# Attention on pairs of heads with features on partitions, and pooling moved to the second projections

## The reference

```python
def gqa_attend(qb, k, v):
    s = jnp.einsum('bqhgd,bkhd->bhgqk', qb, k, preferred_element_type=jnp.float32) * HEAD_DIM ** -0.5
    p = jax.nn.softmax(s, axis=-1)
    return jnp.einsum('bhgqk,bkhd->bqhgd', p.astype(v.dtype), v)
...
    mix = jnp.concatenate([pool_mixer(p, w_pool, s_pool),
                           gla_output(o_gl, gg, g_gla, x.dtype),
                           latent_attention(ql, k_all, v_all)], axis=-1) @ w_out
```

## Time and profile before

| what | us |
|---|---|
| median of 3 runs | 2187.87 |
| lowest, highest | 2180.58, 2188.46 |
| the profiled execution | 2186.37 |
| its span on the core | 2184.6 |
| PE busy (share) | 1962.4 (90%) |
| DVE, ACT, POOL busy | 1141.4, 908.6, 318.5 |

### The profile page before, as it was taken

One profiled execution on the slowest core, in us unless ns is written; L12 is line 12 of the kernel. 1 busy time (PEld: TensorE's weight loads), 2 busy tenths in 40 slices (PEclk: granted clock), 3 DMA queues, 4 the chain that ended last, 5 costly groups with the idle time before them and its releaser, 6 DMA issues.

```text
span 2184.6 us, 28958 instructions
## 1 busy us (share of the span) xinstructions
PE 1962.4 (90%) x12175; PEld 1679.3 (77%) x12175; DVE 1141.4 (52%) x1623; ACT 908.6 (42%) x1404; POOL 318.5 (15%) x359
## 2 busy tenths in 40 slices
PE   4888778999999999869989977988899999988999
PEld 2766457788888888745788967878789978868997
DVE  2544447545466455564355545764355546565553
ACT  3543334344445544533354534433244435434443
POOL 1011013211131122120121110021200004300000
PEclk8998688999999999977789988989899999989999
DMA  7445253453546566432345533420055554503554
GB/s 266 138 155 192 95 195 97 155 164 132 167 157 212 193 211 197 137 114 78 122 146 187 181 127 98 134 77 20 25 164 182 185 184 163 184 20 116 179 187 136
DMA packets 217869, 320.59 MB, mean 147 GB/s; under 512 B 8454, under 2 KB 123850, under 8 KB 217356
## 3 DMA queue, kind: packets, MB, share of 16 engines
q1 hardware_dynamic: 212532, 308.96, 42.9%
q0 software_dynamic: 1744, 6.03, 0.8%
q10 hardware_dynamic: 3464, 3.75, 0.5%
HBM read 317.68 MB, written 1.05 MB: 146 GB/s over the span
## 4 chain that ended last, share of the span: by engine, by line
PE 74%; DVE 12%; ACT 6%; DMA 3%; issue 3%; POOL 2%; SPq 0%; POOLq 0%; ACTq 0%; DVEq 0%
PE ps L69 70%; DVE WLO L86 3%; PE ps L77 3%; DVE AR L96 2%; ACT WHI L80 2%; DVE AR L86 2%; DMA RAW<-in_w_mod_dram 1%; ACT AR L80 1%; POOL SM L86 1%; ACT PMD L80 1%; DMA RAW<-in_w_in_dram 1%; DVE SM L99 1%; ACT XR L80 1%; ACT TH L80 1%; POOL XR L86 1%
## 5 line engine op out<-in xcount | busy, mean ns | idle before, releaser
L86 DVE TENSOR_TENSOR WLO<-RAW,WHI 128x1024 fp32r<-128x1024 f32 (+3 forms) x506 | 591.4, 1211 | 426.0 <-ACT WHI L80 425.9
L80 ACT ACTIVATE WHI<-RAW 128x1024 fp32r<-128x1024 f32 (+3 forms) x506 | 488.7, 1015 | 388.0 <-PE ps L69 316.3
L69 PE MATMUL ps<-TH,WHI 128*128 128x256 f32 x1664 | 482.8, 290 | 24.9 <-DVE WLO L86 17.1
L69 PE MATMUL ps<-TL,WHI 128*128 128x256 f32 x1664 | 477.5, 287 | 0.0
L69 PE MATMUL ps<-TH,WLO 128*128 128x256 f32 x1664 | 477.4, 287 | 0.0
L69 PE MATMUL ps<-WHI,ARR 128*128 128x512 f32 x1120 | 357.6, 395 | 2.6 <-DVE ARR L86 1.5
L69 PEld LDWEIGHTS ps<-TH,WHI 128*128 128x128 f32 x1664 | 326.5, 196 | 34.9 <-issue 22.5
L69 PEld LDWEIGHTS ps<-TL,WHI 128*128 128x128 f32 x1664 | 326.7, 196 | 0.2
L69 PEld LDWEIGHTS ps<-TH,WLO 128*128 128x128 f32 x1664 | 326.1, 196 | 0.0
L69 PE MATMUL ps<-WHI,TH 128*128 128x512 f32 (+3 forms) x624 | 246.4, 395 | 29.8 <-DVE WLO L86 23.4
L69 PEld LDWEIGHTS ps<-WHI,ARR 128*128 128x128 f32 x1120 | 211.7, 189 | 55.2 <-issue 8.9
(11 more groups left out here) (170 smaller groups left out, 2025.0 us busy)
## 6 DMA issues: line engine op xcount, KB each, us to landing
RAW<-in_w_mod_dram SPq DMA_DIRECT2D x48, 1024.0 KB, 5.3
RAW<-in_w_up_dram SPq DMA_DIRECT2D x48, 1024.0 KB, 5.4
RAW<-in_w_down_dram SPq DMA_DIRECT2D x48, 1024.0 KB, 5.2
RAW<-in_ffn_w_in_dram SPq DMA_DIRECT2D x44, 1024.0 KB, 5.1
RAW<-in_w_in_dram SPq DMA_DIRECT2D x20, 1024.0 KB, 5.3
RAW<-in_ffn_w_out_dram SPq DMA_DIRECT2D x20, 1024.0 KB, 5.1
RAW<-in_dil_w_in_dram SPq DMA_DIRECT2D x18, 1024.0 KB, 5.0
RAW<-in_gdn_w_in_dram SPq DMA_DIRECT2D x16, 1024.0 KB, 5.8
```

The source lines that it names most:

```text
L69: return Made(None if self.eng is None else self.eng.matmul(o, l, r, start=start, stop=stop))
L80: return Made(None if self.eng is None else self.eng.activation(o, i, f, **k))
L86: return Made(None if self.eng is None else self.eng.tensor_tensor(o, a, b, op))
```

## The change

- Attention goes by pairs of heads (v = 0 and 1, the two key heads) in 8 steps plus a tail of 4. The two scores of a pair are issued one behind the other on the two halves of the array's rows. For sequence 0 both go into one bank (256 keys each), so the second waits for the first; one maximum and one copy then serve the pair. For sequence 1 they have a bank each.
- The product with the values is turned over: 64 value columns are stationary and the 128 transposed exps move, so that the result has features on partitions, the two heads of a pair on the two halves of the array's columns. The transposes `at` are gone. The reciprocal sums, which now must lie along the free axis, are spread by 8 matmuls per query tile (key `rs`, `ps<-CF,SM` 64x128), copied by ACT into `attended`, and multiplied in by DVE; ACT and DVE split the result as before.
- The output weights' lower 512 rows must be in the order of the new partitions: their tile of `w_out` is loaded by two transfers of 64 partitions each.
- Pooling's second product takes all four 64x64 quarters in one bank, and DVE and ACT work on 128 partitions at once (2 scalings, 1 split each, where there were 4 and 2).
- In `common_order` both poolings of layer 0 begin in the second projections (three of four steps there, the fourth first in the next stage), attention (0, 0) has 12 of its 36 steps there, and attention (0, 1) is `slow`.

The core of the diff, 8 columns of indentation taken off:

```diff
@@ -341,8 +341,14 @@
-        src = src[128 * t.k0:128 * (t.k0 + t.nk), t.c0:t.c0 + t.n].rearrange("(k p) n -> p k n", p=128)
-        sp.dma(t.of(t.raw), src).then_inc(w_land[t.i % NRAW], t.i)
+        src = src[128 * t.k0:128 * (t.k0 + t.nk), t.c0:t.c0 + t.n]
+        if (t.name, t.k0) == ("w_out", 4):
+            for v in range(2):
+                sp.dma(t.of(t.raw)[64 * v:64 * v + 64], src[256 * v:256 * v + 256].rearrange("(a d) n -> d a n", a=4)).then_inc(
+                    w_land[t.i % NRAW], t.i)
+        else:
+            sp.dma(t.of(t.raw), src.rearrange("(k p) n -> p k n", p=128)).then_inc(w_land[t.i % NRAW], t.i)
@@ -738,6 +744,7 @@
+PTBOTH = AR[:, 9984:11008].rearrange("p (v n) -> p v n", v=2)
@@ -966,128 +973,176 @@
...
+STEPS = [(qt, a) for qt in range(2) for a in range(4)]
+TAIL = 4
+def last_of(step):
+    return divmod(step, 4)[0] if 0 <= step < len(STEPS) and step % 4 == 3 else None
...
+def att_key(kind, l, sq, step, v):
+    return kind, l, sq, step, v * sq
+def att_of(kind, l, sq, step, v):
+    b = banks.of(att_key(kind, l, sq, step, v))
+    return b if sq == 1 else b[:, 256 * v:256 * v + 256]
+def att_take(kind, l, sq, step, v):
+    if v == 0 or sq == 1:
+        banks.take(att_key(kind, l, sq, step, v), aring)
+        wait_free(att_key(kind, l, sq, step, v))
+    return att_of(kind, l, sq, step, v)
+def att_pb(sq, step, v):
+    if sq == 0:
+        return PBb[step % 3][:, 256 * v:256 * v + 256], (step - 3, v)
+    return PBb[(2 * step + v) % 3], divmod(2 * step + v - 3, 2)
...
+    nk = 2 + 2 * sq
+    for step in range(len(STEPS) + TAIL):
+        if step < len(STEPS):
+            qt, a = STEPS[step]
+            pe.wait_ge(act_pj, ("qt", l, 2 * sq + qt))
...
+            for v in range(2):
+                p = slice(64 * v, 64 * v + 64)
+                b = att_take("s", l, sq, step, v)
+                if (sq, v) == (0, 1):
+                    pe.wait_ge(pe_at, ("s", l, sq, step, 0))
+                pe.matmul(b, QT[sq][p, a, 128 * qt:128 * qt + 128], KT[p, 0:128 * nk], True, True).then_inc(pe_at, ("s", l, sq, step, v))
...
+        if 0 <= u < len(STEPS):
+            qt, a = STEPS[u]
+            key = ("o", l, 2 * sq + qt)
+            if a == 0:
+                banks.take(key, oring)
+                wait_free(key)
+            b = banks.of(key)
+            for e in (act_at, dve_at):
+                if ("p", l, sq, u) in e.at:
+                    pe.wait_ge(e, ("p", l, sq, u))
...
+                for v in range(2):
+                    m = pe.matmul(b[64 * v:64 * v + 64, 128 * a:128 * a + 128], UA[:, i, 64 * v:64 * v + 64],
+                                  PTb[v][:, 128 * i:128 * i + 128], i == 0, i == nk - 1)
...
+        yield
+        u = step - 1
+        if 0 <= u < len(STEPS):
+            for v in range(2):
+                b = att_take("pt", l, sq, u, v)
+                pe.wait_ge(act_at, ("e", l, sq, u, v))
+                for i in range(nk):
+                    m = pe.transpose(b[:, 128 * i:128 * i + 128], att_pb(sq, u, v)[0][:, 128 * i:128 * i + 128], IDN)
+                m.then_inc(pe_at, ("pt", l, sq, u, v))
+        yield
+        if (i := last_of(step - 1)) is not None:
+            ti = 2 * sq + i
+            b = banks.take(("rs", l, ti), ring)
+            wait_free(("rs", l, ti))
+            pe.wait_ge(dve_at, ("rc", l, ti))
+            for h in range(8):
+                p, a = slice(64 * (h // 4), 64 * (h // 4) + 64), h % 4
+                m = pe.matmul(b[p, 128 * a:128 * a + 128], s_at[i][:, 16 + h:17 + h].broadcast_to([128, 64]), IDN, True, True)
+            m.then_inc(pe_at, ("rs", l, ti))
+        yield
+def act_exp(l, sq, step, v):
+    qt, a = STEPS[step]
+    h = 4 * v + a
+    to, (u, uv) = att_pb(sq, step, v)
+    act.wait_ge(dve_at, ("mx", l, sq, step, v * sq))
+    if u >= 0:
+        act.wait_ge(pe_at, ("pt", l, sq, u, uv))
+    free = [("free", att_key("s", l, sq, step, v))] if sq == 1 or v == 1 else []
+    act.act(to, att_of("s", l, sq, step, v), ACT.Exp, bias=s_at[qt][:, h:h + 1], accum_out=s_at[qt][:, 8 + h:9 + h]).then_inc(
+        act_at, ("e", l, sq, step, v), *free)
...
+    for step in range(len(STEPS) + TAIL):
+        if step < len(STEPS):
+            act_exp(l, sq, step, 0)
+            if sq == 0:
+                act_exp(l, sq, step, 1)
+        yield
+        if sq == 1 and step < len(STEPS):
+            act_exp(l, sq, step, 1)
+        u = step - 1
+        if 0 <= u < len(STEPS) and (sq == 1 or u % 2 == 0):
+            free = ("free", att_key("pt", l, sq, u, 0))
+            act.wait_ge(pe_at, ("pt", l, sq, u, 1 - sq))
+            if u >= 1:
+                act.wait_ge(pe_at, ("o", l, sq, u - 1))
+            if sq == 1:
+                act.act(PTb[0], banks.of(("pt", l, sq, u, 0)), ACT.Copy).then_inc(act_at, free, ("p", l, sq, u))
+            else:
+                act.act(PTBOTH[:, :, 0:256], banks.of(("pt", l, sq, u, 0)).rearrange("p (v n) -> p v n", v=2), ACT.Copy).then_inc(
+                    act_at, free, ("p", l, sq, u))
+        yield
+        if (i := last_of(step - 1)) is not None:
+            ti = 2 * sq + i
+            act.wait_ge(pe_at, ("rs", l, ti))
+            act.act(attended(l, ti), banks.of(("rs", l, ti)), ACT.Copy).then_inc(act_mx, ("free", ("rs", l, ti)), ("rs", l, ti))
+        if (i := last_of(step - 3)) is not None:
+            ti = 2 * sq + i
...
+            act.wait_ge(dve_mx, ("ao", l, ti))
+            act.act(MH[:, 4:8, 128 * ti:128 * ti + 128], h4(attended(l, ti)), ACT.Copy).then_inc(act_mx, ("at", l, ti))
...
+    for step in range(len(STEPS) + TAIL):
+        if step < len(STEPS):
+            qt, a = STEPS[step]
+            mx = s_at[qt][:, 0:8].rearrange("p (v a) -> p v a", v=2)[:, :, a]
+            dve.wait_ge(pe_at, ("s", l, sq, step, 1 - sq))
+            if sq == 0:
+                b = banks.of(("s", l, sq, step, 0)).rearrange("p (v n) -> p v n", v=2)
+                dve.reduce(mx, b, ALU.max, negate=True).then_inc(dve_at, ("mx", l, sq, step, 0))
+            else:
+                dve.reduce(mx[:, 0:1], banks.of(("s", l, sq, step, 0)), ALU.max, negate=True).then_inc(dve_at, ("mx", l, sq, step, 0))
+                dve.wait_ge(pe_at, ("s", l, sq, step, 1))
+                dve.reduce(mx[:, 1:2], banks.of(("s", l, sq, step, 1)), ALU.max, negate=True).then_inc(dve_at, ("mx", l, sq, step, 1))
+        if (i := last_of(step - 1)) is not None:
+            s = s_at[i]
+            dve.wait_ge(act_at, ("e", l, sq, step - 1, 1))
+            dve.reciprocal(s[:, 16:24], s[:, 8:16]).then_inc(dve_at, ("rc", l, 2 * sq + i))
+        yield
+        u = step - 1
+        if 0 <= u < len(STEPS) and (sq == 1 or u % 2 == 1):
+            free = ("free", att_key("pt", l, sq, u, 1))
+            dve.wait_ge(pe_at, ("pt", l, sq, u, 1))
+            if u >= 1:
+                dve.wait_ge(pe_at, ("o", l, sq, u - 1))
+            if sq == 1:
+                dve.copy(PTb[1], banks.of(("pt", l, sq, u, 1))).then_inc(dve_at, free, ("p", l, sq, u))
+            else:
+                dve.copy(PTBOTH[:, :, 0:256], banks.of(("pt", l, sq, u, 0)).rearrange("p (v n) -> p v n", v=2)).then_inc(
+                    dve_at, free, ("p", l, sq, u))
+        yield
+        if (i := last_of(step - 2)) is not None:
+            ti = 2 * sq + i
+            dve.wait_ge(act_mx, ("rs", l, ti))
+            dve.wait_ge(pe_at, ("o", l, sq, step - 2))
+            o = attended(l, ti)
+            dve.tt(o, banks.of(("o", l, ti)), o, ALU.mult).then_inc(dve_mx, ("free", ("o", l, ti)), ("ao", l, ti))
+        if (i := last_of(step - 3)) is not None:
+            ti = 2 * sq + i
...
+            dve.tt(ML[:, 4:8, cs], h4(attended(l, ti)), MH[:, 4:8, cs].bitcast(F32), ALU.subtract).then_inc(dve_mx, ("at", l, ti))
...
@@ -1110,15 +1165,16 @@
-    for hf in range(2):
-        p = slice(64 * hf, 64 * hf + 64)
-        b = banks.take(("pw", l, sq, hf), ring)
-        wait_free(("pw", l, sq, hf))
-        pe.wait_ge(act_mx, ("pm", l, sq))
-        pe.wait_ge(ld_small, "all")
-        for a in range(2):
+    key = ("pw", l, sq)
+    b = banks.take(key, ring)
+    wait_free(key)
+    pe.wait_ge(act_mx, ("pm", l, sq))
+    pe.wait_ge(ld_small, "all")
+    for a in range(2):
+        for hf in range(2):
+            p = slice(64 * hf, 64 * hf + 64)
-        m.then_inc(pe_mx, ("pw", l, sq, hf))
+    m.then_inc(pe_mx, key)
@@ -1126,32 +1182,25 @@
...
+    act.wait_ge(dve_mx, ("ps", l, sq))
+    act.act(MH[:, 0:2, 256 * sq:256 * sq + 256], SCALED[l].rearrange("p (a t) -> p a t", a=2), ACT.Copy).then_inc(
+        act_mx, ("ps", l, sq))
...
+    for a in range(2):
+        m = dve.ts(SCALED[l][:, 256 * a:256 * a + 256], b[:, 256 * a:256 * a + 256], SPC[:, l, a:a + 1], None, ALU.mult)
...
@@ -1648,7 +1697,7 @@
-        engine.wait_ge(pe_mx, ("at", l, 2 * sq + 1))
+        engine.wait_ge(dve_mx, ("at", l, 2 * sq + 1))
@@ -3002,7 +3051,7 @@
     return iter(())
 
-ATTENTION = 3 * (len(UNITS[0]) + TAIL)
```

(16 more changed lines are left out.)

123 lines of the change are left out of this document (9 added, 114 removed).

## The result

The changed kernel takes 2151.89 us (median of 4 runs, 2142.42 to 2154.24), the kernel before beside it 2187.11 (4 runs, 2180.58 to 2188.46): a ratio of 0.984 (0.980 to 0.987). The forecast was 2150 in 2131 to 2180, faster. The profiled execution has a span of 2151.0 us against 2184.6, so 33.6 us less, where the steps of the forecast summed to 36.6. The sum is right; two of its five terms are not, and it is luck that their errors cancel.

A forecast was written before the change was run, and what follows sets the result against it. The prediction took PE as the bound in sequence 0's work and the last attention stage, the first attention stage being loosest. Its terms, +10.2 - 15.7 - 14.9 - 17.2 + 1.0 = -36.6 from 2186.4, gave 2150 us, range 2131 to 2180.

The forecast's parts named there:

- Work of sequence 0: Stage up to layer 1's `w_in`: PE-bound, cheaper scores and products less `rs`, -14.9 us, bounds -15 and -6.
- the sign come that was named for this stage: From attention (0, 1)'s first score to the end of that stage's work, some 15 us less.
- The split loads: Two 64-partition transfers for the lower `w_out` tile, three times 0.3 us for the second issue: +1.0 us (0 to +7).
- the 7.4 of the prediction: Two 512 KB halves of a `w_out` tile, 3.7 us each, landing one behind the other: end at 7.4 us.
- Second projections: Pooling moved here delays a `w_in` tile and adds PE work: +10.2 us (+4 to +14).
- First attention stage: Pooling products and waits leave, some costs come back, products with the values get cheaper: -15.7 us (-22 to -8).
- The 4.15 us wait: First attention stage: a wait at pooling's end comes back because `rs` meets DVE's queued GLA work, 4.0 us.
- Last attention stage: Scores -9.7, products -8.9, pooling -2.9, `rs` +1.3, bank waits +3: together -17.2 us (-23 to -5).
- the bank waits: Last attention stage: a pair's step takes four banks of three, so PE waits for exps and copies: +3 us (0 to 15).
- No overlap of the columns: Rival: column halves don't overlap in the new forms, products save nothing and `rs` costs more: 2175 us, chance 0.07.
- Latency in PE's place: Rival: the loop through three banks and GLA's chain limit the last and first attention stages: 2169 us, chance 0.17.
- Half clock: Rival: less work between the same waits puts PE at 1.2 GHz throughout both attention stages: 2196 us, slower, chance 0.07.

The follow-up runs named there:

- e3: The changed kernel with the second score of every sequence 1 pair waiting for the first; ratio 0.990 to the kernel before.
- e1: The changed kernel with heads a and 4+(a^1) paired, so w_out keeps its row order and its lower tile loads in one transfer; ratio 0.979 to the kernel before.
- e10: The changed kernel with crossed head pairs, one w_out lower-tile load, GLA (0, 1) at its old pace, attention (0, 1) steps at two slots; 2140.97 us.
- e8: The changed kernel with crossed head pairs, one w_out lower-tile load, old GLA (0, 1) pace, attention (0, 1) at two slots, four last-stage banks; ratio 0.979 to before.
- e4: The changed kernel with each pair's products with the values issued head by head instead of alternating; ratio 0.983 to the kernel before.
- e5: The changed kernel with layer 0's pooling steps all back in the first attention stage, its halves still merged; ratio 0.987 to the kernel before.
- e7: The changed kernel with four banks instead of three for scores and transposes in the last attention stage, GLA keeping two; ratio 0.984 to the kernel before.
- e9: The changed kernel run again unaltered on another chip group; 2145.97 us, ratio 0.982 to the kernel before.

## Why the prediction was right, and where it was wrong

**Work of sequence 0: the step that failed.** "PE-bound at full clock: -8.7 - 7.2 + 1.0" took the window from 453.3 to 622 for the whole stage. There PE is the bound, and e3 shows that it is. But from 308.8 to 453.3 PE had idled 18.7 us before, behind GLA, the norm and the first tiles, and the edit of the weave changed the order there as well: PE idles 27.0 us ahead of the first score in the changed kernel, 24.6 in e1, 20.3 in e10. The prediction had said that the "sync points between PE and them halve", and priced the new stream lengths at nothing. They cost about 4 us (e8 and e10 against e1), the wait for POOL's PMD first of all. Of the terms themselves the scores were right (-8.4), the products too large: two heads took 1.7 us from start to start before, not 2.0, so -5.2. `rs` was twice too small (+2.0 for +1.0), because its order uses one half four heads long (e4). All other rows together make 2.4, ahead of the first score, where the granted clock fell from 0.89 to 0.85; behind it the clock is 1.00 in both. About 2 us of the new idle time have no experiment of their own (e10 has 24.5, the kernel before 22.3). Nor did the sign come that was named for this stage: from the first score up to layer 1's `w_in` it is 6.3 us less, not 15.

**The split loads.** +1.0 was forecast, +2.1 measured (e1), inside the 0 to +7. The row that the prediction lacked is that of a half of 64 partitions: 5.1 us for the first of a pair, the pair whole 7.4 after its first issue. That is the 7.4 of the prediction, though not by its working of two times 3.7; at this stage's start it was 8.7, where one transfer took 6.5. The Trainium skill, DMA: Bandwidth & Descriptors, Rules for kernel authors, says that such halves "serialize". The runs agree that the split gains nothing, and show that here it costs 2.2 to 2.4 us.

**Second projections.** +4.3 for +10.2. The chain behind `pm` was right: 5.3 of load and 2.3 of splits forecast, 7.7 taken, with a wait of 5.1 us that stands where it was expected. Its start was wrong: I had a pair, GLA and a `pm` of 3.7 us at half clock ahead, used at 140.2; `pm` took 2.00 at full clock and was done at 136.8. The tile came 2.4 us later than before (1.0 of it from ahead of the first cut) instead of 5.9. And pooling as a whole cost this part 6.4 (e5), where the forecast's pieces made 11.0.

**First attention stage.** -18.5 for -15.7. The move of pooling is worth 12.8 (e5), and the halves merged, 7.0 to 3.1 us in their rows, another 3.9: 16.7, for which the forecast's 22.6 - 3.0 - 4.0 = 15.6 is close. The 4.15 us wait that I let come back did not: `rs` waits for nothing over 0.3 us.

**Last attention stage.** -18.5 for -17.2, inside the stage's own spread of 86.6 to 90.4. Scores -9.9 (forecast -9.7), products -10.7 (-8.9), pooling's rows -2.9 (-2.9 with the wait); `rs` +3.0 (+1.3), again its order in part; the bank waits were 5.3 us for +3 (e7), so the loop was read rightly and sized low. The forecast left out all other rows, which are 3.8 us shorter at a granted clock of 0.84 instead of 0.74; idle time is up by 5.7.

**The rivals.** No overlap of the columns (2175) is refuted by 1.09 us a pair, and half of it is true when eight records of a half stand in a row. Latency in PE's place (2169) needed 103 us in the last stage and 74 in the first; they took 89.7 and 63.2, with ACT at 34 and DVE at 48 of 90. The Trainium skill, TensorEngine Tiling (Array Packing), PSUM Bottleneck, says that the copy out of PSUM may become the bottleneck after a fourfold speedup of TensorE; the prediction took that for halves too, where the page doesn't say it. The runs don't bear the rival out here: what they show of it are 5.3 us, and a bank removes them. Half clock (2196) did not come: the granted clock rose in both attention stages, from 0.69 to 0.77 (0.74 in e9) and from 0.74 to 0.84.

**Slips in its sums.** 147.8 less 142.1 is 5.7 us, not 5.9. The rival without overlap says 1.5 us more for each `rs` and adds up 1.0. The upper bounds of the stages make -5 only without the load's +7; with it the range would have ended near 2188.

So 2150 came true because the work of sequence 0 gave 13.1 us less than forecast and the three others of the four stages 10 more. Nothing in the prediction ties these two together: that the sum came out is luck.

## What to carry to other kernels

Take the price of a new order for itself: when a stream of steps gets another number of slots, every step in the stage meets its producers at another time, and a stage whose middle is bound by one engine is not bound by it at its ends. Give pairs of tiles on halves of the array to the queue by turns: four records of a half in a row cost nothing here, eight cost half of the overlap. And before a load is split to suit a new layout, look whether the heads can be paired so that the old layout stays.

## What the runs showed of the hardware that I had not expected

Overlap of the two column halves depends on the order of issue: 16 records of 128 columns take 1.09 us by turns and 1.58 with eight of a half in a row (e1, e4), while eight records take 0.66 by turns and 0.67 with four of a half in a row (e4, sequence 0).

Of two loads of 64 partitions and 512 KB, issued one behind the other, the first takes 5.1 us, as long as one of 128 partitions and 1024 KB, and the pair 7.4 (6.7 is the median of all twelve halves, each from its own issue).

The same code gets another clock from one execution to the next. The windows of the changed kernel and of e9 that begin near the same instructions of the unchanged rest have the same busy time, but 205 matmul records in one and 238 in the other, at a granted clock of 0.88, a mixture of 1.2 and 2.4 GHz, and of 1.00. First the changed kernel, window and one row of PE's timeline:

```profile
1480.00:1510.00 30.00, 26.86 (x205) 26.23 (x204) 11.49 (x27) 10.09 (x29) 5.31 (x4) 0.88 0.01 1
...
1498.20 3.33 PE L77 MATMUL ps<-CF,AR 128*128 128x128 f32 x16
```

then e9, the same code again:

```profile
1478.30:1508.30 30.00, 26.86 (x238) 26.23 (x236) 11.48 (x27) 12.07 (x34) 5.30 (x4) 1.00 0.01 1
...
1493.90 1.92 PE L77 MATMUL ps<-CF,AR 128*128 128x128 f32 x16
```

Behind this place e9 is 5.0 us ahead, and 7.0 behind a second one near 1895. That is the step between the two rests of 1114.9 and 1107.7 in the table. How much of the spread of a kernel's runs it makes isn't shown, since only one execution of each has a trace; why the clock fell in one and not in the other, the rows don't tell.
